# The last RMSNorm's scaling of a hybrid encoder step, split between GpSimd and VectorE

## The reference, cut to what matters

```python
def rmsnorm(x, w):
    xf = x.astype(jnp.float32)
    y = xf * lax.rsqrt(jnp.mean(xf * xf, axis=-1, keepdims=True) + NORM_EPS)
    return (y * w.astype(jnp.float32)).astype(x.dtype)
...
    h = h + peer_ffn(rmsnorm(h, norm2_w), peer_w_q, peer_sub_keys, peer_u, peer_v)
...
    y_prompt = rmsnorm(hp, final_norm_w)
    y_sample = rmsnorm(hs, final_norm_w)
```

## Time and profile before

| what | value |
|---|---|
| median of three runs | 2234.67 us (2233.51 to 2237.74) |
| the profiled execution's own time | 2248.32 us |
| its span, first to last instruction | 2246.5 us |
| TensorE busy | 2162.1 us, 96% of the span |
| VectorE, ScalarE, GpSimd busy | 57%, 39%, 40% |
| mean granted clock of TensorE | 0.983 |

### The profile page before, as it was taken

The page is one execution under the profiler, slowest core; times in us unless marked ns, Lnnn a source line. Parts: engine busy times, 40 slices in busy tenths (PEclk is TensorE's granted clock), DMA queues, the critical chain, the costliest instruction groups (busy, mean ns, idle before and its releaser), DMA issues.

```text
span 2246.5 us, 41950 instructions
## 1 busy us (share of the span) xinstructions
PE 2162.1 (96%) x16703; PEld 2065.5 (92%) x16703; DVE 1279.8 (57%) x2471; ACT 884.3 (39%) x1722; POOL 901.0 (40%) x555
## 2 busy tenths in 40 slices
PE   8997888998999999999999999999999999999997
PEld 7996777887999999999999999999989999999996
DVE  5353655657699897799611111111356666666666
ACT  5235445524333333799722222222323232333332
POOL 2433344432445545211233333333465555555310
PEclk9999999999999999999999999999999999999999
DMA  4538366624566666377776667667488888888862
GB/s 148 188 114 242 88 190 188 192 83 169 164 192 191 184 194 211 117 226 227 234 283 242 240 237 259 242 234 267 159 274 284 278 277 280 283 276 280 281 229 81
DMA packets 298806, 478.86 MB, mean 213 GB/s; under 512 B 31168, under 2 KB 227584, under 8 KB 298504
## 3 DMA queue, kind: packets, MB, share of 16 engines
q1 hardware_dynamic: 276104, 409.25, 54.9%
q0 software_dynamic: 22528, 67.19, 9.7%
HBM read 383.86 MB, written 159.60 MB: 242 GB/s over the span
## 4 chain that ended last, share of the span: by engine, by line
PE 73%; DVE 2%; DMA 1%; ACT 1%; issue 1%; POOL 0%; SPq 0%; DVEq 0%; ACTq 0%; POOLq 0%
PE banks L126 22%; PE banks L128 22%; PE banks L127 22%; PE banks L2279 4%; PE banks L1968 1%; DMA u_raw<-arg_u 1%; DVE n_y L342 0%; DMA scratch_gates<-gate_stage 0%; DVE res_x L2767 0%; DVE res_lo L349 0%; DVE n_sq L383 0%; DVE n_inv L335 0%; DVE gates_in L2764 0%; ACT res_hi L1823 0%; ACT wout_wh L1779 0%
## 5 line engine op out<-in xcount | busy, mean ns | idle before, releaser
L126 PE MATMUL banks<-res_hi,u_high 128*128 128x288 f32 x1456 | 439.0, 301 | 3.1 <-POOL u_low L2156 2.1
L128 PE MATMUL banks<-res_hi,u_low 128*128 128x288 f32 x1456 | 429.7, 295 | 0.0
L127 PE MATMUL banks<-res_lo,u_high 128*128 128x288 f32 x1456 | 429.5, 295 | 0.0
L128 PE MATMUL banks<-w_high,v_low 128*128 128x448 f32 x1024 | 374.7, 366 | 3.3 <-issue 3.3
L126 PE MATMUL banks<-w_high,v_high 128*128 128x448 f32 x1024 | 374.9, 366 | 1.0 <-issue 0.5
L127 PE MATMUL banks<-w_low,v_high 128*128 128x448 f32 x1024 | 374.9, 366 | 0.4 <-issue 0.4
L2156 POOL TENSOR_TENSOR u_low<-u_raw,u_high 128x1024 fp32r<-128x1024 f32 x75 | 181.2, 2416 | 305.8 <-ACT u_high L2152 305.8
L2685 DVE TENSOR_TENSOR gated<-gelu_out,gates_in 128x448 f32<-128x448 f32 x76 | 48.1, 634 | 410.2 <-ACT gelu_out L2642 392.4
L126 PEld LDWEIGHTS banks<-res_hi,u_high 128*128 128x128 f32 x1456 | 274.2, 188 | 3.6 <-POOL u_low L2156 2.3
L127 PEld LDWEIGHTS banks<-res_lo,u_high 128*128 128x128 f32 x1456 | 274.3, 188 | 0.1
L128 PEld LDWEIGHTS banks<-res_hi,u_low 128*128 128x128 f32 x1456 | 273.7, 188 | 0.0
(11 more groups left out here) (424 smaller groups left out, 4579.2 us busy)
## 6 DMA issues: line engine op xcount, KB each, us to landing
scratch_v_rows<-arg_v SPq DMA_DIRECT2D x128, 512.0 KB, 8.0
v_raw<-scratch_v_rows SPq DMA_DIRECT2D x128, 512.0 KB
u_raw<-arg_u SPq DMA_DIRECT2D x37, 1024.0 KB, 6.3
scratch_gates<-gate_stage SPq DMA_DIRECT2D x14, 2048.0 KB, 7.6
scratch_prod<-gated SPq DMA_DIRECT2D x128, 224.0 KB, 2.9
w_raw<-scratch_prod SPq DMA_DIRECT2D x128, 224.0 KB
q_raw<-arg_u SPq DMA_DIRECT2D x38, 512.0 KB, 4.1
gates_in<-scratch_gates SPq DMA_DIRECT2D x19, 896.0 KB, 5.1
```

The source lines that it names most:

```text
L126: pe.matmul(out, ah, bh, start=first, stop=False)
L127: pe.matmul(out, ah, bl, start=False, stop=False)
L128: return pe.matmul(out, al, bh, start=False, stop=last)
```

## The change

The first half of the columns is now scaled by two other engines. ScalarE multiplies each block's first half by the norm's weight, in place, behind the square of the next block (`weigh_first`; the last block's behind the root). VectorE inverts both halves of the root one after the other, with a tick of `inverted` each, waits for both, and multiplies the second half only. GpSimd waits for the first reciprocal, and then multiplies the weighed first half of each block by the inverse root (`pool_last`, behind `pool_rows` in its stream). SP's stores alternate: two blocks of the second half, the same two blocks of the first half, and so on. The count and the size of the stores stay.

```diff
+        inverted, weighed, scaled_first = core.sem("last_inverted"), core.sem("last_weighed"), core.sem("first_half_scaled")
...
-            for half in range(2):
-                for n in range(4):
-                    c = slice(SP + half * DN // 2, SP + (half + 1) * DN // 2)
-                    sp.wait_ge(scaled, half * DT + 2 * n + 2)
+            for n in range(4):
+                for half, ready in ((1, scaled), (0, scaled_first)):
+                    c = half_of(half, SP)
+                    sp.wait_ge(ready, 2 * n + 2)
                     sp.dma_start(a["y"][:, 2 * n:2 * n + 2, c], acts.x[:, 2 * n:2 * n + 2, c]).then_inc(stored, 16)
...
                 act.activation(square_of(dt), acts.x[:, dt, cols], ACT.Square).then_inc(squared, 1)
+                if dt:
+                    weigh_first(act, dt - 1)
             act.wait_ge(sums, 1)
             act.activation(root, out_bank(0), ACT.Sqrt, bias=core.eps[:, 0:1], scale=1.0 / D_MODEL).then_inc(rooted, 1)
+            weigh_first(act, DT - 1)
+
+        def weigh_first(act, dt):
+            act.wait_ge(squared, dt + 1)
+            x = acts.x[:, dt, half_of(0, SP)]
+            act.activation(x, x, ACT.Copy, scale=core.norms[:, 2, dt:dt + 1]).then_inc(weighed, 1)
...
             for half in range(2):
-                h = slice(half * DN // 2, (half + 1) * DN // 2)
-                c = slice(SP + half * DN // 2, SP + (half + 1) * DN // 2)
-                core.chains["dve"].on(dve)(dve.reciprocal(inv[:, h], root[:, h]))
-                for dt in range(DT):
-                    x = acts.x[:, dt, c]
-                    dve.scalar_tensor_tensor(out=x, in0=x, scalar=core.norms[:, 2, dt:dt + 1], in1=inv[:, h],
-                                             op0=ALU.mult, op1=ALU.mult).then_inc(scaled, 1)
+                h = half_of(half)
+                dve.reciprocal(inv[:, h], root[:, h]).then_inc(inverted, 1)
+            dve.wait_ge(inverted, 2)
+            h, c = half_of(1), half_of(1, SP)
+            for dt in range(DT):
+                x = acts.x[:, dt, c]
+                dve.scalar_tensor_tensor(out=x, in0=x, scalar=core.norms[:, 2, dt:dt + 1], in1=inv[:, h],
+                                         op0=ALU.mult, op1=ALU.mult).then_inc(scaled, 1)
+
+        def half_of(half, first=0):
+            return slice(first + half * DN // 2, first + (half + 1) * DN // 2)
+
+        def pool_last(pool):
+            h, c = half_of(0), half_of(0, SP)
+            pool.wait_ge(inverted, 1)
+            for dt in range(DT):
+                pool.wait_ge(weighed, dt + 1)
+                x = acts.x[:, dt, c]
+                pool.tensor_tensor(x, x, inv[:, h], ALU.mult).then_inc(scaled_first, 1)
...
                 pool_rows(pool)
+                pool_last(pool)
```

## The result

The changed kernel took 2245.98 us in the median of 22 runs (2237.17 to 2260.04), the kernel before 2238.14 beside it (22 runs, 2232.78 to 2251.3): ratio 1.0035, with a 95% interval of 1.0018 to 1.0052, so 4.0 to 11.6 us slower. The forecast was no change that can be measured, 2235.0 in a range of 2232.0 to 2238.0. Some 3.5 us of the distance to 2245.98 lie in the kernel before itself, whose median was 2234.67 in the three runs shown first; the loss beside it stands.

What follows compares the result with a forecast made beforehand. TensorE, busy 96% of the span, was taken to bound the kernel; the change touches only the 11.53 us tail. ScalarE 0, VectorE -0.67, issue +0.37, queue +0.6 make +0.3 on 2234.67: 2235.0 us, range 2232.0 to 2238.0.

Steps and rivals of the forecast that it cites:

- a change of R by over 3 us: Tail, VectorE's first reciprocal behind the root to span's end, 11.53 us before: a change over 3 us refutes the prediction.
- ScalarE's weighing, nothing: ScalarE behind the squares and root: eight scaled copies, 0.45 us each, fit into gaps and cost nothing.
- The reciprocals and GpSimd's start: Tail: VectorE's two reciprocals run back to back, 2234.97 to about 2238.05; GpSimd starts 0.09 us after the first, at 2236.61.
- A GpSimd product of 128x224, 0.63 us and 0.59 from start to start: GpSimd's tail: duration and pitch of one two-tensor product alone, from rows at 512 and 1024 columns.
- a choice that no row bore out: Tail: VectorE's second reciprocal was taken not to hold up GpSimd, which does three products during it, to 2238.42.
- The two together, a pair of 0.79: Tail products on GpSimd and VectorE: each VectorE product adds 0.20 us to GpSimd's pitch of 0.59.
- the strict rival: Tail: GpSimd and VectorE exclude each other for whole durations, pairs 1.08 us, 1.15 to 2.05 slower, 2236.4; chance 0.12.
- They don't run beside each other: Tail: claim that GpSimd's and VectorE's products interlock, one VectorE product passing between two of GpSimd.
- The sum of +0.3, the stores in it: Tail total: VectorE -0.67, one more store issue behind the last product +0.37, store queue +0.6, ScalarE 0.
- the queue's term: Stores at the end: the last four bunch and queue on nearly full transfer engines, 0.6 us (two thirds of 0.9).
- Nothing stands behind them: GpSimd's stream: claim that the new products queue behind nothing and are followed by nothing, so no cost was counted.
- The third rival: GpSimd's first tail product starts late after rest and indirect fetches, about 6 us for freshly loaded code, 2238.0; chance 0.04.

Runs made afterwards that it cites:

- e1: Changed kernel with its last block closed without GpSimd's drain; ratio to the kernel before 0.9996 (0.9966 to 1.0027).
- e0: The changed kernel itself, run again unaltered beside the others on one chip; ratio to the kernel before 1.0025 (1.0000 to 1.0051).
- e9: Against the kernel before: ScalarE weighs both halves; GpSimd, drained early, does two first-half products beside the second reciprocal, VectorE the other products; ratio 0.9995.
- e5: Changed kernel without GpSimd's 256 indirect fetches, leaving out the picked experts of the first 128 tokens; not timed, first reciprocal to span's end 12.2 us.
- e8: Changed kernel with one more GpSimd drain right behind its indirect fetches, timed with 12 runs; ratio to the kernel before 1.0011 (0.9984 to 1.0037).
- e4: Changed kernel with one more GpSimd drain right behind its indirect fetches; not timed, first reciprocal to span's end 12.0 us.
- e3: Kernel before, with GpSimd also clearing one spare column when VectorE's last product is done; ratio to the kernel before 1.0026 (1.0000 to 1.0051).
- e6: Changed kernel with 128 value fetches kept, the 128 row fetches and their VectorE addition left out; not timed, first reciprocal to span's end 16.8 us.
- e7: Against the kernel before: ScalarE weighs both halves, VectorE multiplies plainly, no GpSimd in the tail, stores in the old order; ratio 1.0018 (0.9991 to 1.0044).

## Why the prediction was wrong

By the sign that the prediction itself gave, a change of R by over 3 us, it is wrong: R grew by 5.2. Step by step, each time counted from the start of the first reciprocal and the forecast in brackets:

- **ScalarE's weighing, nothing:** right. One weighing took 0.47 us (0.45), no table load came, and VectorE's idle times ahead of its last two additions were 0.20 and 0.67 us, as before. From the last addition to the first reciprocal it is 3.74 us (2226.60 to 2230.34), against 3.75 before (2231.22 to 2234.97):

```profile
2226.60 0.62 DVE L2766 TENSOR_TENSOR res_x<-banks,res_x 128x448 f32<-128x448 f32 x1 [0.67 <-PE banks L128]
```

- **The reciprocals and GpSimd's start:** right. The two reciprocals took 2.97 us (3.08), and GpSimd started at 1.64 (1.64), which is 2231.98.
- **A GpSimd product of 128x224, 0.63 us and 0.59 from start to start:** right. The second to the fifth:

```profile
2232.60 0.65 POOL L2789 TENSOR_TENSOR res_x<-res_x,gates_in 128x224 f32<-128x224 f32 x1
2233.21 0.65 POOL L2789 TENSOR_TENSOR res_x<-res_x,gates_in 128x224 f32<-128x224 f32 x1
2233.82 0.80 POOL L2789 TENSOR_TENSOR res_x<-res_x,gates_in 128x224 f32<-128x224 f32 x1
2234.59 0.80 POOL L2789 TENSOR_TENSOR res_x<-res_x,gates_in 128x224 f32<-128x224 f32 x1
```

  The first of these rows lies wholly beside the second reciprocal, which ends at 2230.34 + 2.97 = 2233.31: 0.65 us, 0.61 to the next. That the reciprocal leaves GpSimd alone was a choice that no row bore out, and it holds.
- **The two together, a pair of 0.79:** right in size. From the fourth product on, beside VectorE's, GpSimd's pitch is 0.76 (2233.82 to 2234.59), and a VectorE product is open for 0.84 us instead of 0.45 while it waits:

```profile
2234.80 0.84 DVE L2777 SCALAR_TENSOR_TENSOR res_x<-res_x,norms,gates_in 128x224 f32<-128x224 f32 x1
```

  GpSimd loses 0.15 us to each VectorE product, not its whole 0.45: the strict rival gave 1.08 for the pair. "They don't run beside each other" says too much, though: alone they come every 0.61 and every 0.37 us, 0.98 for both in turn, so with 0.76 a pair still overlaps in part. The Trainium skill (SBUF — State Buffer, "SBUF: two separate sides") states that of two such operations the one that starts first holds the shared ports for its whole instruction, and the other waits. The trace agrees in that VectorE's product is held up, not in that GpSimd loses the time of a whole one. VectorE ended at 8.30 (8.40), GpSimd at 7.33 (7.40).
- **The sum of +0.3, the stores in it:** the mechanism was right, one term too small. With the drain away (e1) R is 0.5 more than before (0.3). VectorE ended 0.77 us sooner (0.67). But the last issue came at 9.08 (8.80), as late as before (2234.97 to 2244.06), since issues close behind each other took longer, 0.47 us in the median instead of 0.37: this term is 0.76 and not 0.37. From the last issue to the end e1 took 3.0 us (2241.3 to 2244.3) instead of 2.44, so the queue's term is 0.5 (0.6). The changed kernel's issues:

```profile
L2571 SPq DMA_DIRECT2D out_y<-res_x x8: 372/468/504, 2234.9 to 2239.4; - x8
```

- **"Nothing stands behind them" in GpSimd's stream:** this is the step that failed. The drain that closes the block stands there. Behind the indirect fetches it ends 9.2 us behind GpSimd's last instruction, and the change moved that instruction from 74 us ahead of the first reciprocal into the tail. That put the block's end at 7.33 + 9.23 + 0.2 = 16.8 us, where the stores alone end at 12.1: 4.7 us of the 5.2 that R grew; the other 0.5 is what the forecast had at 0.3. The prediction counted what a lone last store costs to the span's end (2.44 us) and took it for all that lies there; it never asked what else the last block waits for.
- **The third rival** had the right engine, GpSimd behind its indirect fetches, but put the cost ahead of the first product. There nothing was lost: the start came as forecast, and the products beside the reciprocal took 0.65 us each. That its 6 us are of the order of the drain's 9.2 is chance; its price is for something else.

The whole time's 1.0035 (4.0 to 11.6 us) holds the 5.2 us of the tail. Beside it the time outside the span, each run's time less its span, grew: 2.05 to 2.15 us in the 22 runs of the changed kernel, 1.74 to 1.84 in the 75 runs of the kernel before beside e0 to e9. What these 0.3 us are no view shows; they are there without the fetches (e5, 2.06) and with the early drain (e8, 2.06 to 2.16), too. Whether the rest up to the middle of the interval, some 2 us, is scatter, the runs don't settle; the ratios of e1 (0.9996) and e8 (1.0011) leave room for either.

## What to carry to other kernels

Before work moves to an engine that had long been done, read what closes its stream, too: a drain hidden 74 us ahead of the end is free there and can become the end itself. In this kernel a GpSimd stream with indirect fetches owed 9.2 us at its next drain, and an explicit drain where GpSimd is idle paid it off the path to the end (e4). When several engines' ends are compared, measure from a common event to the span's end: R came out within 0.1 us again when a kernel was profiled again (the changed kernel and e0 16.8, e4 and e8 12.0), where the intervals of whole times are 8 to 14 us wide.

## What the hardware showed that I had not expected

- A drain on GpSimd behind indirect fetches ends 9.22 to 9.23 us behind the last instruction when the fetches are 75 to 448 us back (changed kernel, e0, e3, e6), and 10.5 to 10.8 us behind the last fetch when it follows at once (before, e4, e7). Between 128 and 256 fetches it is the same. Without fetches since the last drain it is over 0.07 us behind the last instruction (e4, e5). What GpSimd does in these 9.2 us no view shows, and no run tells whether other transfers that GpSimd issues would cost the same.
- A reciprocal on VectorE and a product of two tensors on GpSimd run side by side at full pace (changed kernel, e9), where a product on each slows both: from 0.61 and 0.37 us to 0.76 from start to start.
